# A second turn for the latent attention's strands in every round of the RWKV mixer

## The reference

```python
sb_cols, mla_cols, rwkv_cols = jnp.split(x @ w_in, ...)
o_sb = merge_heads(stick_breaking_attention(q, k, v))            # 4 heads
o_mla = mla_mixer(mla_cols, ...)                                 # 4 heads: causal softmax attention over 512 keys
o_rwkv = rwkv7_mixer(rwkv_cols, ...)                             # 8 heads: a state carried from token to token
mix = jnp.concatenate([o_sb, o_mla, o_rwkv], axis=-1) @ w_o
```

## Time and profile before

| | us |
|---|---|
| median of 3 runs | 3169.63 |
| lowest and highest | 3164.59, 3176.6 |
| the profiled execution, its own time | 3173.54 |
| its span, first to last instruction | 3171.8 |
| mean granted clock of PE | 0.926 |

### The profile page before, as it was taken

How to read it: one execution, slowest core, us unless ns; L and a number is a source line. 1 busy time by engine, 2 the same in 40 slices (tenths; PEclk the granted TensorE clock), 3 DMA queues, 4 the chain that set the end, 5 groups by cost and what they waited for, 6 DMA issues and landing times.

```text
span 3171.8 us, 45102 instructions
## 1 busy us (share of the span) xinstructions
PE 2869.4 (90%) x19896; PEld 2372.6 (75%) x19896; DVE 1536.6 (48%) x2384; ACT 1000.4 (32%) x1501; POOL 191.1 (6%) x182
## 2 busy tenths in 40 slices
PE   7987999999988999999869779999998777799998
PEld 5876788877877788887638767888876477578887
DVE  3576434344574434333355565343633465564445
ACT  3333323233333332223243224232333422233322
POOL 0200000000100000000012300000000133100000
PEclk9968999999967999999979889999999788899999
DMA  4101222222002222321000023222220000123221
GB/s 157 63 1 50 92 94 93 98 76 93 27 1 95 90 93 93 106 85 67 1 0 3 30 105 107 95 92 99 80 78 14 1 2 30 68 94 106 93 93 67
DMA packets 30724, 216.59 MB, mean 68 GB/s; under 512 B 3648, under 2 KB 3776, under 8 KB 6080
## 3 DMA queue, kind: packets, MB, share of 16 engines
q1 hardware_dynamic: 30528, 213.69, 19.2%
HBM read 211.58 MB, written 2.10 MB: 67 GB/s over the span
## 4 chain that ended last, share of the span: by engine, by line
PE 81%; DVE 13%; ACT 4%; issue 1%; DMA 0%; DVEq 0%; SPq 0%; ACTq 0%
PE PS L531 78%; PE PS L534 3%; DVE SC L1245 2%; DVE R L1245 1%; DVE SM L1256 1%; DVE SM L1245 1%; ACT LN L1989 1%; ACT SPL L1989 1%; DVE X L1253 1%; DVE SPL L1245 1%; DVE HA L1245 1%; PE PS L1030 1%; PE PS L1080 0%; ACT R L1989 0%; DVE SM L1253 0%
## 5 line engine op out<-in xcount | busy, mean ns | idle before, releaser
L531 PE MATMUL PS<-H,SPL 128*128 128x512 f32 (+1 forms) x4560 | 1055.1, 392 | 10.0 <-DVE SPL L1245 5.4
L531 PEld LDWEIGHTS PS<-H,SPL 128*128 128x128 f32 (+1 forms) x4560 | 852.4, 188 | 195.8 <-issue 10.3
L1245 DVE TENSOR_TENSOR SPL<-RAW,SPL 128x2048 fp32r<-128x2048 f32 (+2 forms) x194 | 434.0, 2240 | 738.2 <-ACT SPL L1989 738.1
L1989 ACT ACTIVATE SPL<-RAW 128x2048 fp32r<-128x2048 f32 (+2 forms) x194 | 361.7, 1870 | 887.2 <-PE PS L531 847.8
L531 PE MATMUL PS<-SPL,Uu 128*128 128x512 f32 x2592 | 589.8, 389 | 0.0
L531 PEld LDWEIGHTS PS<-SPL,Uu 128*128 128x128 f32 x2592 | 486.6, 188 | 101.0
L531 PE MATMUL PS<-SPL,H 128*128 128x512 f32 (+2 forms) x2112 | 463.6, 381 | 26.1 <-DVE SPL L1245 25.3
L531 PEld LDWEIGHTS PS<-SPL,H 128*128 128x128 f32 x2112 | 389.4, 193 | 99.7 <-issue 27.5
L1989 ACT ACTIVATE R<-PS 128x512 f32<-128x512 f32 (+2 forms) x182 | 104.7, 585 | 268.6 <-PE PS L531 242.1
L1245 DVE TENSOR_TENSOR X<-X,PS 128x512 f32<-128x512 f32 x112 | 76.7, 685 | 108.2 <-PE PS L531 108.2
L1245 DVE TENSOR_TENSOR Uu<-R,Uu 128x512 fp32r<-128x512 f32 x108 | 74.8, 693 | 79.5 <-ACT Uu L1989 79.5
(11 more groups left out here) (218 smaller groups left out, 2610.0 us busy)
## 6 DMA issues: line engine op xcount, KB each, us to landing
RAW<-in_wA SPq DMA_DIRECT2D x84, 1024.0 KB, 4.8
RAW<-in_wB SPq DMA_DIRECT2D x84, 1024.0 KB, 4.8
RAW<-in_wAo SPq DMA_DIRECT2D x8, 1024.0 KB, 4.8
RAW<-in_wBo SPq DMA_DIRECT2D x8, 1024.0 KB, 6.4
LN<-in_ln SPq DMA_DIRECT2D x4, 1024.0 KB, 5.8
P<-in_pB SPq DMA_DIRECT2D x2, 1920.0 KB, 8.7
RAW<-in_wBm SPq DMA_DIRECT2D x4, 704.0 KB, 4.1
X<-in_x SPq DMA_DIRECT2D x4, 512.0 KB, 5.2
```

The source lines that it names most:

```text
L531: return pe.matmul(out, l_, r_, start=start, stop=stop)
L1245: return v.tensor_tensor(out, a, b, o)
L1989: return a.activation(out, in_, f, scale=scale)
```

## The change

In the list that `turns` gets, both strands stand twice, in front of `features(l)` and behind it. It is the same generator object in both places, so it takes two of its steps in each round; nothing is computed twice. This is done on all four compute engines, and nothing else is changed:

```diff
-                turns(latent(l), stick_, strand(2, UNITS_B[2]), strand(3, UNITS_B[3]), features(l),
+                latent_heads = [strand(2, UNITS_B[2]), strand(3, UNITS_B[3])]
+                turns(latent(l), stick_, *latent_heads, features(l), *latent_heads,
                       *[prep(l, t) for t in range(4)], scan(l), *[post(l, t) for t in range(4)])
```

More of the change, by code:

```diff
@@ L2669, in gpsimd @@
                 flags.clear()
-                turns(latent(l), idle(4, "sb"), strand(2), strand(3), features(l), *[prep(l, t) for t in range(4)],
-                      scan(l), *[post(l, t) for t in range(4)])
+                latent_heads = [strand(2), strand(3)]
+                turns(latent(l), idle(4, "sb"), *latent_heads, features(l), *latent_heads,
+                      *[prep(l, t) for t in range(4)], scan(l), *[post(l, t) for t in range(4)])
                 fence()
```

## The result

The changed kernel takes 3178.49 us (median of 20 runs, 3163.93 to 3190.99), the kernel before 3166.15 us in the same session (20 runs). The ratio is 1.0039, with a 95% interval of 1.0021 to 1.0057: some 12 us slower, where 18 us faster was forecast. By the bound of 0.5% that the prediction set this is no change, but the interval leaves out 1, and the time lies above the predicted range of 3122 to 3173.

What follows compares the result with a forecast made beforehand. It took PE-full stretches to alternate with half-empty ones, features being DVE-bound; terms summed to -9.1 us a layer, -18 in two, so 3151.5 us against the median of 3169.6, with a range of 3122 to 3173.

Steps and rivals of the forecast that it cites:

- Features, +9.5: In the features, attention work ahead of the path on ACT and DVE makes `prep` start 9.5 us later a layer.
- The five terms behind the four products: End of features: exponentials, copies, product, transposes and last copy of unit 2, about 8.8 us before `prep` instead of 5.3.
- Head and levels of tiles 0 and 1, -1: Levels of tiles 0 and 1: attention work leaving and coming in is nearly even, -1 us, bounds -2 and +1.
- Tail -8: Tail of tiles 0 and 1, now between levels of tiles 2 and 3: gaps filled, 22 us becomes 14.
- head of tiles 2 and 3 -24.6: Head and first level round of tiles 2 and 3, between levels: 34 us becomes 9.4 of PE's own work.
- The bound I set from POOL: Merged head of tiles 2 and 3: POOL's masks hold PE up for 3 us at worst, making the gain -21.6.
- Levels of tiles 2 and 3, 0: Levels of tiles 2 and 3: PE is full before and after, so no change.
- Last stretch, +15: Behind the last levels: norms of tiles 0 and 1 beside the tail of tiles 2 and 3, +15 us, bounds +7 and +21.
- the gap of 5 to 10 us: Last stretch: PE stands still about 5 to 10 us while DVE does the first turn of `post` for both tiles.
- the new waits eat it all: Rival: last stretch +21 and features +13 cancel the gains, 0 a layer, 3170 us; chance 0.2.
- The clock rival: Rival: PE starts the levels of tiles 0 and 1 at its low clock, up to 30 us more a layer; chance 0.1.
- nearly all of the hiding comes off: Rival: features only +4 and last stretch only +7, so -22.6 us a layer, 3124 us; chance 0.2.

Runs made afterwards that it cites:

- e1: The changed kernel, but the attention's second turn begins only when the features have ended; 3184.1 us, ratio 1.0065 to the kernel before.
- e2: The changed kernel, but tiles 2 and 3 and the norms held until round 36, where they stood before; 3181.1 us, ratio 1.0040 to the kernel before.
- e7: The changed kernel with the second turn behind `prep` and `prep` in tile order 2, 3, 0, 1; 3167.5 us, ratio 1.0018 to the kernel before.
- e6: The changed kernel with the attention's second turn placed behind the steps of `prep`; 3172.9 us, ratio 1.0024 to the kernel before.
- e15: The changed kernel with the norms (`post`) of tile 1 started in round 39 instead of 34; 3168.1 us, ratio 1.0004 to the kernel before.
- e12: The kernel before, with norms of tile 0 from round 40 and tile 1 from 45; 3157.6 and 3155.0 us, ratios 0.9974 and 0.9961.
- e11: The kernel before, with norms of tiles 0 and 1 both from round 40 instead of 36; 3175.8 us, ratio 1.0028 to the kernel before.
- e16: The kernel before, with norms of tile 0 from round 36, as it was, and tile 1 from 41; 3160.2 us, ratio 0.9976.

## Why the prediction was wrong, step by step

- *Features, +9.5: right.* The first product of `prep` stands 80.1 us into the stage instead of 71.0, +9.1. (The five terms behind the four products, 2.4, 1.5, 2.89, half of 3.84 and 0.6, add up to 9.3 and not to 8.8, which would make it +10.) What the walk did not see is that the doubled units cost as much outside the features (e1).
- *Head and levels of tiles 0 and 1, -1: wrong in sign.* e2 shows the term alone: from the first product of `prep` to the end of the levels (the `HA,LN` product behind them) it is 53.1 us, and 52.1 before, so +1, the bound. The wait for exponentials in the levels (2.9 us) is new; the waits for DVE in the head (2.9 and 1.1) are not, since before they were 2.3 and 1.1. Of the tail's -8, e2 gives the 4 of the attention.
- *Tail -8, head of tiles 2 and 3 -24.6, together -32.6: the step that failed.* "Between levels it costs PE only its own work at full clock" treats a merged round as if engines could take whatever is ready. They are in order, so a round lasts as long as its hand-overs. The stretch from the first product of `prep` to the end of the levels got 20.3 us shorter and not 33.6: 13 us a layer of the forecast went to the waits listed above. The bound I set from POOL (3 us) was on the wrong engine: DVE and the issue gaps (5.6 of the 16.2 us) held PE up, and the issue gaps had no term at all. Shown for DVE's order by e7 against e6 (3.2 us a layer) and for the merging as a whole by e2 (it brought 1.2 us, not 13.6); what each single wait is worth is read from the timeline alone.
- *Levels of tiles 2 and 3, 0: nearly right.* 43.5 of 46 us busy at a clock of 1.00; the 2.5 us between are issue gaps.
- *Last stretch, +15: right in place and close in size.* It ended 50 us behind the levels instead of 33, +17. The mechanism was named ("stands behind tile 1's `g2` product, which waits for `po_z`") but priced as part of the norms; e15 showed that the pair of norms in one round is 5 of it, and can be had back. The size is in part luck: the gap of 5 to 10 us that was forecast for the first turn of `post` came as waits of 2.4, 0.9 and 0.9 us, and the longest wait that was new was the 6.0 on `po_z`.
- *Sum.* 9.1 - 20.3 + 17 = +6 in the profiled first layer, where -9.1 was forecast.
- *Rivals.* The second, "the new waits eat it all", was nearest: its 3170 us with both its bounds, where the waits in the middle were missing too. The clock rival was not what happened: the granted clock was 0.85 to 0.93 in the stretches from 1689 to 1754, but 1.00 in the pure levels of tiles 2 and 3. That nearly all of the hiding comes off had no support.

On interleaving, the Trainium skill (Perfetto Trace Analysis, Optimization Strategy) says that mixing regimes with different bounds may improve a kernel. Here that held for one tile's norms beside full levels (e12), and not for two tiles' (e11).

What stays open: why the merged rounds have more issue gaps, how the 4 us that remain of the stage in the changed kernel divide between waits and the clock, and why the whole kernel's time went up by 12 us where the two stages explain 8. A second bank for the `g2` product, which would take the wait away without a stagger, was not tried.

## What to carry to other kernels

When two half-empty stretches are merged on in-order engines, do not price the result by the busiest engine's work. Walk one merged round through the engines, and count each hand-over and each wait that now has other chains behind it. Before moving work, look for twins in one round (two tiles, one buffer between them): setting them a few rounds apart was one edit, and worth more here than the whole reordering. And where the profile names no releaser, look at what the instruction queues do just before.

## What the hardware showed that I had not expected

- PE stood still for 0.3 to 4.0 us in the middle of groups of 64x64 products, at a DMA share of 0.02 as well as at 0.31, and each time went on 1.2 to 1.6 us behind the end of a 16 KB packet of instructions.
- A group of 128 products that took 3.90 us in the levels took 6.66 behind a wait of 4.06 us (e11, at a granted clock of 0.56 from 1776 to 1783), and the `g2` product took 1.13 us behind a wait of 0.85 and 2.08 behind one of 6.03. In the changed kernel the granted clock was 0.66 in the 10 us around 1825.
- Much of the scatter of 20 us and more between runs lies ahead of the second block, which starts between 1596 and 1618 us, while the two stages of a profile agree within 1 us in most. In single layers a stage was up to 7 us longer (237.2 against 233.0 before, 235.3 against 228.1 in e16). The runs' granted clock goes with their time: in the last session, of the kernel before, 0.938 at 3140.4 us and 0.922 at 3178.2.
